# One 512-column matmul for the high weights, and VectorE adds the two halves of a bank

## The reference, cut to what matters

```
h = rms_norm(x, g) @ w_in            # 6672 outputs: gated linear attention (gla) and dilated attention
x = x + mixed @ w_out
xt @ w_query                         # then top-k over product keys
u = expert_down[...]; act = gelu(u . xt); out = (gates * act) @ expert_up
for layer in (pool mixer, recurrent LRU mixer):
    uz = rmsnorm(x) @ w_in_2         # 8192 outputs: u and z
    y = mixer(u) * silu(z);  o = y @ w_out_2
    x = x + rmsnorm(o);  gate = sigmoid(rmsnorm(x) @ w_gate);  e = p @ w_ple
    x = x + rmsnorm(e * gate)
```

## Time and profile before

| what | value |
|---|---|
| time, median of 2 runs | 3404.3 us (3401.87 to 3406.74) |
| span of the profiled execution, first to last instruction | 3399.5 us |
| TensorE clock granted, mean | 0.999 of full |
| TensorE matmul, busy | 3377.7 us (99%) |
| VectorE, busy | 2285.7 us (67%) |
| ScalarE, busy | 1663.9 us (49%) |

### The profile page before, as it was taken

How to read it: one execution, slowest core, us unless ns; L and a number is a source line. 1 busy time by engine, 2 the same in 40 slices (tenths; PEclk the granted TensorE clock), 3 DMA queues, 4 the chain that set the end, 5 groups by cost and what they waited for, 6 DMA issues and landing times.

```text
span 3399.5 us, 66556 instructions
## 1 busy us (share of the span) xinstructions
PE 3377.7 (99%) x29384; PEld 3355.2 (99%) x29384; DVE 2285.7 (67%) x3023; ACT 1663.9 (49%) x1789; POOL 134.9 (4%) x132
## 2 busy tenths in 40 slices
PE   9999999999999999999999999999999999999999
PEld 9999999999999999999999999999999999999998
DVE  5777679986655555555555577788646778787466
ACT  5545444455544344344444453333445677777455
POOL 0000000144400000000000000000000000000000
PEclk9999999999999999999999999999999999999999
DMA  6445455566676665655566645555554545555543
GB/s 253 159 140 186 176 214 186 187 217 210 217 237 219 216 220 206 230 189 196 198 214 221 207 173 207 190 195 186 199 199 176 200 162 199 199 181 192 204 181 137
DMA packets 125328, 669.45 MB, mean 197 GB/s; under 512 B 11056, under 2 KB 44592, under 8 KB 47344
## 3 DMA queue, kind: packets, MB, share of 16 engines
q1 hardware_dynamic: 88224, 623.44, 52.0%
q10 hardware_dynamic: 36816, 41.75, 3.7%
HBM read 643.39 MB, written 20.97 MB: 195 GB/s over the span
## 4 chain that ended last, share of the span: by engine, by line
PE 94%; DVE 3%; ACT 1%; issue 1%; DMA 0%; ACTq 0%; SPq 0%; DVEq 0%
PE PS L558 30%; PE PS L559 30%; PE PS L560 30%; PE PS L857 2%; DVE WL L1555 1%; ACT WH L1050 1%; DVE A L1579 0%; DVE WX L1555 0%; PE PS L573 0%; PE PS L748 0%; PE PS L733 0%; PE PS L839 0%; DVE OO L2100 0%; DVE XT L2106 0%; PE PS L701 0%
## 5 line engine op out<-in xcount | busy, mean ns | idle before, releaser
L1555 DVE TENSOR_TENSOR WL<-RAW,WH 128x2048 fp32r<-128x2048 f32 x576 | 1318.6, 2290 | 811.2 <-ACT WH L1050 809.0
L558 PE MATMUL PS<-A,WH 128*128 128x256 f32 x5536 | 1544.6, 279 | 7.4 <-DVE A L1579 5.1
L560 PE MATMUL PS<-A,WL 128*128 128x256 f32 x5536 | 1531.6, 277 | 0.0
L559 PE MATMUL PS<-A,WH 128*128 128x256 f32 x5536 | 1531.6, 277 | 0.0
L1050 ACT ACTIVATE WH<-RAW 128x2048 fp32r<-128x2048 f32 x576 | 1102.1, 1914 | 843.6 <-PE PS L560 830.5
L558 PEld LDWEIGHTS PS<-A,WH 128*128 128x128 f32 x5536 | 1041.8, 188 | 11.9 <-issue 4.4
L559 PEld LDWEIGHTS PS<-A,WH 128*128 128x128 f32 x5536 | 1040.3, 188 | 0.7
L560 PEld LDWEIGHTS PS<-A,WL 128*128 128x128 f32 x5536 | 1040.1, 188 | 0.0
L558 PE MATMUL PS<-CO,WH 128*128 128x256 f32 x2048 | 565.2, 276 | 0.0
L559 PE MATMUL PS<-CO,WH 128*128 128x256 f32 x2048 | 565.2, 276 | 0.0
L560 PE MATMUL PS<-CO,WL 128*128 128x256 f32 x2048 | 565.2, 276 | 0.0
(11 more groups left out here) (305 smaller groups left out, 2930.8 us busy)
## 6 DMA issues: line engine op xcount, KB each, us to landing
RAW<-in_w_in SPq DMA_DIRECT2D x175, 1024.0 KB, 4.8
RAW<-in_peer_down SPq DMA_DIRECT2D x128, 1024.0 KB, 4.8
RAW<-in_peer_up SPq DMA_DIRECT2D x128, 1024.0 KB, 5.3
RAW<-in_w_out SPq DMA_DIRECT2D x80, 1024.0 KB, 4.7
RAW<-in_w_gate SPq DMA_DIRECT2D x32, 1024.0 KB, 4.8
RAW<-in_w_query SPq DMA_DIRECT2D x16, 1024.0 KB, 4.8
gates_away<-XT ACTq DMA_DIRECT2D x16, 1024.0 KB, 8.1
RAW<-in_pool_w SPq DMA_DIRECT2D x16, 1024.0 KB, 4.8
```

Source lines behind the costliest of these rows:

```text
L558: e.matmul(ps, wh, x[:, k, 0, :], start=first, stop=False, skip_group_check=True)
L559: e.matmul(ps, wh, x[:, k, 1, :], start=False, stop=False, skip_group_check=True)
L560: return e.matmul(ps, wl, x[:, k, 0, :], start=False, stop=last, skip_group_check=True)
L1555: e.tensor_tensor(W_LOW[c], RAW[:, c % NRAW, :], W_HIGH[c].bitcast(F32), ALU.subtract).then_inc(s_lo, 1)
```

## The change

`is_wide(c)` says which chunks are done in the new way: 385 of the 589. Not wide are the chunks of expert_up and w_ple (their banks hold two tiles), w_query and the first 36 of expert_down, the last three of the attention inputs, the last one of several stages, and the gate weights of the LRU layer. Wide are all 13 of gla, 33 of attention, 15 of w_out, 35 and 55 of expert_down, all 80 of the pool layer, 30 of each output projection, 15 of each gate, and 64 of the LRU layer: 385 chunks, 6160 blocks.

For a block of a wide chunk one matmul of 512 columns takes the high weights against high and low activations side by side and writes the whole bank; one of 256 columns takes the low weights against the high activations and adds to the first half. So two weight loads and two matmuls stand where three of each stood, with the same 768 columns in all. The first half of the bank then holds high·high + low·high, the second half high·low, and VectorE must add the two when it takes the tile out:

- `scaled` and the pool_w tiles: a `tensor_reduce` over the two halves (512 elements in, 256 out) into the destination, a wait of VectorE on its own semaphore `s_joined`, then the multiplication as before, now from SBUF.
- w_out: a second `tensor_tensor` add to XT, with the same wait between the two.
- output projection: VectorE reduces the bank into OO and frees it (`s_osum`); ScalarE squares OO, waits for that, and then scales OO in place. Before, ScalarE read the bank and freed it.

```
+    def product(e, key, c, b, x, k, first, last):
+
+        if not is_wide(c):
+            return block(e, psum(key), c, b, x, k, first, last)
+        wh, wl = W_HIGH[c][:, b * 128:b * 128 + 128], W_LOW[c][:, b * 128:b * 128 + 128]
+        both, full = x[:, k, :, :].rearrange("p a t -> p (a t)"), BANK[bank[key]][:, :]
+        if last:
+            e.matmul(psum(key), wl, x[:, k, 0, :], start=False, stop=False, skip_group_check=True)
+            return e.matmul(full, wh, both, start=False, stop=True, skip_group_check=True)
+        e.matmul(full, wh, both, start=first, stop=False, skip_group_check=True)
+        return e.matmul(psum(key), wl, x[:, k, 0, :], start=False, stop=False, skip_group_check=True)
...
-            ins = block(e, psum(c), c, b, x, b, b == 0, b == 15)
+            ins = product(e, c, c, b, x, b, b == 0, b == 15)
...
         for i in range(16):
-            plan(("o", l, i), next(turn), s_sq, 16 * (3 + 4 * l) + i + 1)
+            if i < 15:
+                plan(("o", l, i), next(turn), s_osum, 15 * l + i + 1)
+            else:
+                plan(("o", l, i), next(turn), s_sq, 16 * (3 + 4 * l) + i + 1)
...
+                e.wait_ge(s_osum, 15 * l + i + 1)
+                square(e, m, i, OO[:, i, :])
+                e.wait_ge(s_sq, 16 * m + i + 1)
+                e.activation(OO[:, i, :], OO[:, i, :], ACT.Copy, scale=vec("g_post_2", 16 * l + i))
...
+    def both(key, p1=128):
+        return BANK[bank[key]][0:p1, :].rearrange("p (a t) -> p t a", a=2)
+
+    def joined(e, dst, key, p1=128):
+
+        e.tensor_reduce(dst, both(key, p1), AX.X, ALU.add).then_inc(s_joined, 1)
+        n_joined["n"] += 1
+        e.wait_ge(s_joined, n_joined["n"])
+
     def scaled(e, c, dst, m, p1=128):
 
         e.wait_ge(s_used, c + 1)
+        if is_wide(c):
+            joined(e, dst, c, p1)
+            e.wait_ge(s_r, 2 * m + 2)
+            e.tensor_tensor(dst, dst, R[0:p1, :], ALU.mult).then_inc(s_ev, 1)
+            return
         e.wait_ge(s_r, 2 * m + 2)
         e.tensor_tensor(dst, psum(c)[0:p1], R[0:p1, :], ALU.mult).then_inc(s_ev, 1)
...
+            if is_wide(c):
+                e.tensor_tensor(XT[:, n, :], XT[:, n, :], psum(c, 1), ALU.add).then_inc(s_joined, 1)
+                n_joined["n"] += 1
+                e.wait_ge(s_joined, n_joined["n"])
             e.tensor_tensor(XT[:, n, :], XT[:, n, :], psum(c), ALU.add).then_inc(s_ev, 1)
...
+            for i in range(15):
+                if O_END[l][i] + 1 == c:
+                    e.wait_ge(s_used, c)
+                    e.tensor_reduce(OO[:, i, :], both(("o", l, i)), AX.X, ALU.add).then_inc(s_osum, 1)
```

More of the change, by code:

```diff
@@ L248, in vec, with is_wide @@
         return VEC[p0:p1, o:o + 1]
+    NARROW = ([(C_WO - 3, C_WO), (C_WO + 15, C_D0 + 36), (C_U0 - 1, C_D1), (C_D1 + 55, C_L[0])]
+              + [(C_O[l] + 30, C_G[l]) for l in range(2)] + [(C_G[l] + 15, C_G[l] + 16) for l in range(2)]
+              + [(C_L[1] + 9 * g + 8, C_L[1] + 9 * g + 9) for g in range(8)])
+    def is_wide(c):
+        return not any(c0 <= c < c1 for c0, c1 in NARROW)
     order = []
@@ L945, in pe_oproj @@
                 for b in range(16):
-                    ins = block(e, psum(("o", l, i)), c, b, Y, 16 * hf + b, hf == b == 0, hf == 1 and b == 15)
+                    ins = product(e, ("o", l, i), c, b, Y, 16 * hf + b, hf == b == 0, hf == 1 and b == 15)
                 ins.then_inc(s_used, 1)
```

31 lines of the change are left out of this document (19 added, 12 removed).

## The result

The changed kernel takes 3520.7 us (median of 2 runs, 3519.61 to 3521.84), against 3404.3 before: ratio 1.0342, 95% interval 1.0312 to 1.0372. It is slower by 116 us. The span of the profiled execution is 3518.3 us, 118.8 more than before.

The account below looks back on a forecast made before the run. TensorE was taken to bound the kernel, through the distances between matmul starts. TensorE -17, pool +13, LRU +12 and the others +3 gave +11 us on 3404.3, so 3415 us, with an eight-in-ten range of 3340 to 3470.

Parts of the forecast that it names:

- TensorE's term: Over the 6160 wide blocks, TensorE was to gain 17 us, with +19 and -73 us as ends.
- What bounds the kernel: TensorE, busy 99% of the span: 113.3 ns per 256-column matmul, of which 6.6 ns lie beyond the columns' 106.7.
- TensorE, the step that failed: In wide blocks a 512-column matmul was taken at 224 ns, making a block 337.3 ns.
- its ends: Bounds on TensorE's wide blocks: 343.3 ns, +19 us in all, and 328.3 ns, -73 us.
- Rival 4: In wide blocks, 512-column matmuls fall into the slower 240 ns rhythm for good: +81 us on TensorE, 3500 us; chance 0.05.
- Rival 3 in its second form: VectorE bounds LRU and pool, with 512-column matmuls at 230 to 240 ns: 3490 to 3520 us; chance 0.05.
- VectorE's price: Taking out wide tiles: 356 reduces at about 0.69 us, 244 us, plus 6 us of second adds in w_out.
- Pool: Pool's groups 2 and 3: late low weights stall TensorE by 5 and 8 us, 13 us together, between 6 and 22.
- LRU: Low weights of each LRU group's last chunk come late: +1.5 us per group, 12 us over 8 groups.
- The others: w_out 2 us, first wide expert_down chunk and gates 1 us or less each, attention and output projection nothing: 3 us together.
- Without new waits: Attention, expert_up and the output projections were to show no new waits; expert_down after its first chunks was to lose nothing.

Follow-up runs that it names:

- experiment 2: The kernel before with the change's two matmuls per wide block, tiles taken out as before from the first half, high·low left out: 3468.6 us, ratio 1.0195.
- experiment 4: The kernel before, with high-weight matmuls of 128 to 512 columns in the second expert_down stage only, alternating or grouped: 3381.6 us, one run.
- experiment 6: The kernel before, with other operand forms in the second expert_down stage only (64-column weights, high and low tokens in turn, others): 3434.0 us, one run.
- experiment 9: The kernel before, with matmuls in the second expert_down stage reading tokens in other orders, from 2, 4, 8 or 16 places in turn: 3548.2 us, one run.
- experiment 11: The change with each matmul of a weight product reading its tokens from two places in turn (0, 128, 1, 129, ...): 3448.0 us, ratio 1.0134.
- experiment 1: The change with three 256-column matmuls per block, high·low going to the bank's second half, so only VectorE's and ScalarE's part remains: 3494.8 us, ratio 1.0270.
- experiment 7: The change with the pool and LRU input stages done as before, 241 chunks staying wide: 3450.3 us, ratio 1.0129.
- experiment 10: The kernel before with every weight product's tokens read from two places in turn and sorted back on reading PSUM: 3352.4 us, ratio 0.9854.

## Why the prediction was wrong

The forecast was 3415 us, the measurement 3521: 106 us more, and outside 3340 to 3470. TensorE's term had the wrong sign, and VectorE's was too small in pool.

- *What bounds the kernel: right.* TensorE, with starts 113.3 ns apart; and right that the 6.6 ns beyond 106.7 decide the change.
- *TensorE, the step that failed.* The sum took 224 ns for 512 columns, as a part of the 6.6 ns per instruction and a part per column, and left the short matmul behind it at 113.3. Measured: 235 and 118. Counted in blocks that is +80 us where -17 was forecast, and +68 in the span of experiment 2: the largest part of the error. The 224 lay between a row of the same kind of matmul (230 and 240) and one of another kind (float32, 213). The rows of the same kind were the ones to take, and both of them; the second head's 240 ns was probably a sight of the slow rhythm. (By 230 alone the sum would still have been some 70 us short.) Experiment 4 shows that from 256 columns on the time goes with the columns, experiments 6, 9 and 11 that the order of reading sets how much a column costs. In sequence the 6.6 ns are no price per instruction, and a merge doesn't save them. The differences in this part of the prediction were also taken against 340.2 ns per block, where three times 113.3 are 339.9; that moves its ends to +21 and -71 us and the gain to 16, and changes nothing.
- *Rival 4 named it* (the long matmuls in the slower rhythm for good, +81 us, 3500) and had 0.05 of the chances. It is what experiment 2 shows by itself, with 68 us of span. What it missed is that the short matmuls go along. Rival 3 in its second form (VectorE holds pool and LRU, and the long matmuls take 230 to 240 ns: 3490 to 3520, also 0.05) is the nearest to what happened, though in LRU of the changed kernel VectorE holds little.
- *VectorE's price: right.* 356 reduces at 0.68 to 0.69 us, 239 us more busy time for 250.
- *Pool: right place, size too small.* 13 us forecast (6 to 22), 52.9 measured in experiment 1. The sum gave each u stage 5.7 us of lead to use up, and looked at groups 2 and 3 only. In the trace after, TensorE waits some 2 us in the three chunks behind a pair of pool_w chunks, whose tiles each have their reduce; so no lead is left when the next group's u chunks begin, and all four groups pay (9.9, 9.9, 13.6 and 19.5 us in experiment 1). For the last group 8 x (6.77 - 5.44) = 10.6 us are the u chunks alone.
- *LRU: right.* 12 us forecast as 1.5 per group; experiment 1 has +15.2 and a standstill of 1.35 to 1.56 us ahead of the last chunk of seven groups, and 2.8 in the first. (The sum's own terms, 5.6 less 2.8 and 1, give 1.8 per group, 14 us, which is nearer.) In the change itself the slower matmuls hide most of it: TensorE waits in the first group alone, 2.35 us.
- *The others:* attention, forecast at nothing, has +3.8 in experiment 1, and w_out +4.3 for 2. Expert_down and the output projections have no waits, as said. "Without new waits" holds for expert_down only because the matmuls are slow: the ring of VectorE and ScalarE in the second expert_down stage comes to 5.64 us, right beside their 5.65 and above the 5.40 that was forecast, so it would have held that stage. This was not seen.
- *Adding up:* the forecast added TensorE's and VectorE's terms. They don't add: 68.0 and 98.8 make 118.8. Of the change's 118.8 us, 71.3 lie in pool and LRU, nearly all of which VectorE's part alone would cause (68.1 in experiment 1), and 46.5 (experiment 7) are the other stages, mostly their slower blocks.
- *What can be told apart:* the prediction holds that a change under 2% can't be told from none here. The intervals in this document are 0.2 to 0.3% to either side, so 11 us would have been near the edge, but 50 are clear.

## What to carry to other kernels

A merged matmul saves nothing unless its own time, measured in the same data type and in the same order of reading, is less than that of its parts; where the trace holds an instruction of that kind, its row is better evidence than a split into a price per instruction and one per column. Cost each stage as the longest of its engines and of its rings of hand-overs (here 1.91 + 2.2 + 0.69 + 0.44 + 0.42 us), never as a sum of terms: what makes TensorE faster brings the next ring to light. And before two 256-column matmuls are joined, try reading the operand from two places in turn; it cost here a view on each matmul and on each reader of a bank, and gave 50 us.

## What the runs showed of the hardware

- *Two rhythms.* A 256-column float32r matmul read in sequence takes 113.3 or 117.7 ns from start to start at the full clock, for long stretches (experiment 1, one stage); a 512-column one 231 to 236 ns. What sets it off and ends it was not settled.
- *Fewer columns don't go below 112 ns.* In a row of its kind a matmul with 128 or 192 columns, each with its weight load, takes 112 ns (experiment 4); 256 columns read from two places in turn take 111 to 112, but 109 beside a 512-column one (experiments 9 to 11).
- *The order of the moving operand sets the time.* 256 columns: 111 to 112 ns from two places in turn (512 bytes apart), 113 or 118 in sequence, 143 from four, 220 from eight and sixteen, 230 with a step of 8 bytes. 512 columns: 235 in sequence, 215 to 218 in turn. The Trainium skill (SBUF — State Buffer, "Door 1: The DMA port swizzle", its note on cachelines) says that consecutive accesses to one 16-byte line run at full bandwidth and that each crossing to a new line pays. That bears on the 230 ns; that two places in turn, where every access is to another line than the one before, are the fastest order of all speaks against it as it stands.
- *Half the clock after a standstill.* In the changed kernel TensorE waited 2.35 us for low weights in LRU, and some 1.4 us after its restart the clock fell. The timeline and two windows of it, the standstill and the 4.86 us behind it, with the mean clock third from last:

```profile
2853.24 0.39 PE L570 MATMUL PS<-Y,WH 128*128 128x256 f32 x1 [2.35 <-DVE WL L1582]
...
2855.04 0.41 PE L571 MATMUL PS<-Y,WH 128*128 128x256 f32 x1
2855.25 0.42 PE L572 MATMUL PS<-Y,WL 128*128 128x256 f32 x1
```

```profile
2850.73:2853.24 2.51, 0.16 (x2) 0.00 (x1) 2.51 (x3) 2.23 (x3) 0.00 (x0) 1.00 0.00 0
2853.24:2858.10 4.86, 4.86 (x28) 4.86 (x29) 4.79 (x8) 2.44 (x3) 0.00 (x0) 0.65 0.66 226
```

Some 16 matmuls are 213 ns apart instead of 118, at 1.2 GHz instead of 2.4, and cost 1.6 us on top of the standstill. The same followed a standstill of 2.1 us at one place in pool, 0.2 us after the restart; the other waits in pool, of about 1 us, were not followed by it. A longer standstill need not be either: in experiment 1 TensorE waited 2.6 us at the same place in LRU, and the clock in the 7 us behind it stayed at 1.00.
